# One group of an MLP's second products cut at token 512 in place of token 280

## The reference

```python
def _residual(x, mix, p):
    x = x + _rmsnorm(mix, p['g_post_mix'])
    f = jnp.square(jax.nn.relu(_rmsnorm(x, p['g_pre_mlp']) @ p['w_ff1'])) @ p['w_ff2']
    return x + _rmsnorm(f, p['g_post_mlp'])
```

## Time and profile before

| | |
|---|---|
| median of two runs | 2323.36 us |
| span of the profiled execution, first to last instruction | 2321.0 us |
| what lies around the span, against that median | 2.4 us |
| TensorE matmul busy | 2283.3 us (98%), 17472 records |
| weight loads busy (they overlap matmuls) | 2166.7 us (93%), 17472 records |
| VectorE, ScalarE, GpSimd busy | 916.8, 996.1, 935.4 us |
| mean granted clock of TensorE | 0.998 |

### The profile page before, as it was taken

One profiled execution on the slowest core, in us unless ns is written; L12 is line 12 of the kernel. 1 busy time (PEld: TensorE's weight loads), 2 busy tenths in 40 slices (PEclk: granted clock), 3 DMA queues, 4 the chain that ended last, 5 costly groups with the idle time before them and its releaser, 6 DMA issues.

```text
span 2321.0 us, 41258 instructions
## 1 busy us (share of the span) xinstructions
PE 2283.3 (98%) x17472; PEld 2166.7 (93%) x17472; DVE 916.8 (40%) x1909; ACT 996.1 (43%) x1879; POOL 935.4 (40%) x600
## 2 busy tenths in 40 slices
PE   7999999999999999999999999999999999999997
PEld 7999978889899999999999999788999999999997
DVE  6566555544514401001575664555344153000014
ACT  5444334443555642332344444344345556433412
POOL 2222224444665463544422223144455645545432
PEclk9999999999999999999999999999999999999999
DMA  5122221112124222222321222211222241222222
GB/s 195 54 64 62 85 76 59 57 62 74 62 82 155 68 83 91 82 90 66 118 88 53 72 62 90 70 58 56 72 65 65 82 167 55 83 91 82 90 80 72
DMA packets 59815, 187.89 MB, mean 81 GB/s; under 512 B 8400, under 2 KB 17552, under 8 KB 59120
## 3 DMA queue, kind: packets, MB, share of 16 engines
q1 hardware_dynamic: 51408, 169.28, 22.8%
q10 hardware_dynamic: 8224, 15.97, 1.9%
HBM read 170.99 MB, written 10.89 MB: 78 GB/s over the span
## 4 chain that ended last, share of the span: by engine, by line
PE 92%; DVE 5%; ACT 2%; issue 1%; DMA 0%; POOL 0%; SPq 0%; DVEq 0%
PE dense L941 43%; PE att L941 30%; PE att L1016 2%; PE att L1245 1%; PE att L1156 1%; PE att L1093 1%; PE att L1176 1%; PE att L1283 1%; PE dense L970 1%; PE att L1097 1%; PE att L1079 1%; PE att L1318 1%; DVE h_raw L1912 1%; PE att L1204 1%; PE att L1180 1%
## 5 line engine op out<-in xcount | busy, mean ns | idle before, releaser
L2304 POOL TENSOR_TENSOR wlo<-wraw,whi 128x1024 fp32r<-128x1024 f32 x245 | 588.2, 2408 | 596.9 <-ACT whi L1370 596.9
L941 PE MATMUL dense<-h_hi,whi 128*128 128x280 f32 x1888 | 556.5, 295 | 1.2 <-issue 0.9
L941 PE MATMUL dense<-h_lo,whi 128*128 128x280 f32 x1888 | 550.4, 292 | 0.0
L941 PE MATMUL dense<-h_hi,wlo 128*128 128x280 f32 x1888 | 549.2, 291 | 0.0
L1370 ACT ACTIVATE whi<-wraw 128x1024 fp32r<-128x1024 f32 x302 | 314.9, 1050 | 269.6 <-DMA wraw<-in_w 267.7
L941 PEld LDWEIGHTS dense<-h_hi,whi 128*128 128x128 f32 x1888 | 354.9, 188 | 14.5 <-issue 11.1
L941 PEld LDWEIGHTS dense<-h_hi,wlo 128*128 128x128 f32 x1888 | 354.4, 188 | 0.5
L941 PEld LDWEIGHTS dense<-h_lo,whi 128*128 128x128 f32 x1888 | 354.7, 188 | 0.0
L941 PE MATMUL att<-h_hi,whi 128*128 128x280 f32 x1024 | 299.3, 292 | 0.4 <-issue 0.4
L941 PE MATMUL att<-h_lo,whi 128*128 128x280 f32 x1024 | 298.3, 291 | 0.0
L941 PE MATMUL att<-h_hi,wlo 128*128 128x280 f32 x1024 | 297.8, 291 | 0.0
(11 more groups left out here) (366 smaller groups left out, 4584.3 us busy)
## 6 DMA issues: line engine op xcount, KB each, us to landing
wraw<-in_w SPq DMA_DIRECT2D x302, 512.0 KB, 3.6
x_spill<-x ACTq DMA_DIRECT2D x2, 2240.0 KB, 7.7
x<-x_spill ACTq DMA_DIRECT2D x2, 2240.0 KB, 12.0
k_cat<-k_rope SPq DMA_DIRECT2D x16, 212.0 KB, 3.4
x<-in_x SPq DMA_DIRECT2D x4, 560.0 KB, 6.3
out_y_out<-x SPq DMA_DIRECT2D x4, 560.0 KB, 3.1
out_c_out<-ckv SPq DMA_DIRECT2D x2, 560.0 KB, 5.4
state<-in_state ACTq DMA_DIRECT2D x8, 128.0 KB, 2.0
```

Of the source, the lines that this page charges most:

```text
L941: mm = pe.matmul(bank(u, o, hf)[0:m, :], a[:, k, o * 128:o * 128 + m], b[:, k, H[hf]], start=(k == 0 and i == 0), stop=(k == kt - 1 and i ...
L2304: pool.tensor_tensor(wlo[slot][:, :], wraw[slot][:, :], whi[slot][:, :].bitcast(F32), ALU.subtract).then_inc(pool_done, st.done("pool", f" ...
```

## The change

For `ff2` units 8 to 15 (group 1, in both layers) the two parts of tokens become 0 to 511 and 512 to 559. The six banks are taken at their full width of 512, and `bank` gives the first columns of one, as many as the part has. All other units keep their two parts of 280.

```diff
+CUT = SEQ
...
-        DENSE_BANKS = [dps[0][:, 0:HALF], dps[1][:, 0:HALF]] + [ps[:, b, 0:HALF] for b in (T0, T1, M_, O_)]
+        DENSE_BANKS = [dps[0][:, :], dps[1][:, :]] + [ps[:, b, :] for b in (T0, T1, M_, O_)]
...
+            def parts_of(u):
+                kind, n = UNITS[u]
+                return (slice(0, CUT), slice(CUT, T)) if kind == "ff2" and 8 <= n < 16 else H
...
             def bank(u, o, hf):
-                return bank_of[st.layer, u, o, hf]
+                part = parts_of(u)[hf]
+                return bank_of[st.layer, u, o, hf][:, 0:part.stop - part.start]
...
-                                    mm = pe.matmul(bank(u, o, hf)[0:m, :], a[:, k, o * 128:o * 128 + m], b[:, k, H[hf]],
+                                    mm = pe.matmul(bank(u, o, hf)[0:m, :], a[:, k, o * 128:o * 128 + m], b[:, k, parts_of(u)[hf]],
                                                    start=(k == 0 and i == 0), stop=(k == kt - 1 and i == 2))
...
-                            c = H[hf]
+                            c = parts_of(u)[hf]
```

## The result

The changed kernel takes 2367.07 us (median of two runs, 2366.52 and 2367.62) against 2323.36: 1.0191 times as long, 95% interval 1.0174 to 1.0208. It is slower, as forecast, but by 43.7 us in place of 29.5, and 1.1 us above the top of the range. The interval has 1.02 inside, so whether it is more or less than the two per cent of the prediction isn't decided.

The account below looks back on a forecast made before the run. TensorE's matmuls were taken to bound the kernel; 384 pairs of one wide (224.9 ns) and one narrow (108.5 ns) matmul, 76.8 ns more each, add 29.5 us, from 2323.4 to 2352.9 us, range 2348 to 2366 us.

Parts of the forecast that it names:

- the two per cent of the prediction: Whole kernel: 2% is what a measurement can tell from no change, 46.5 us or 2369.8 us; within it 87%.
- The bound: Group 1: TensorE and weight loads busy end to end, so each nanosecond per matmul reaches the program's end.
- the weights cost nothing: Group 1: slabs are asked for less often, ScalarE and GpSimd have room; VectorE's additions also costed at nothing.
- no wait gave anything back: In or behind group 1: no wait of TensorE that the delay could fill, so nothing comes back.
- The narrow matmul: Group 1's 48-wide matmuls: 108.5 ns each, set by a fresh load of 128 columns; upper bound 128.3 ns.
- The wide matmul: Group 1's 512-wide matmuls: 224.9 ns each, between 215.8 and 234.6 ns.
- today's 11.6 ns: 280-wide matmuls: 128.3 ns less 116.7 ns of streaming; taken as a fixed piece per matmul, not a slower stream.
- the sum: Group 1, both layers: a pair 333.4 ns in place of 256.6, times 384 pairs, +29.5 us.
- The clock: Group 1's narrow runs: no fall of the granted clock in the forecast, since earlier narrow runs stayed at 1.00.
- the clock falls: Rival, group 1: clock drops to 1.2 GHz in narrow runs or next wide runs, 2395 to 2431 us; chance 6%.
- The sign that the prediction names for it: Group 1's window in the new trace: a clock below 1.00 would mean the third rival, the clock falling.
- two thin stretches: Earlier trace: runs of 64-wide and 16-wide matmuls, 4.4 and 2.1 us, alone, where the clock stayed at 1.00.

Follow-up runs that it names:

- The halved load: Changed kernel with group 1's narrow matmuls using 64 of 128 columns of weights; 2336.61 us, 1.0060 times the kernel before.
- the 208 columns: Changed kernel with group 1's narrow part streaming 208 columns, of which the last 48 are taken out; 2355.80 us, 1.0143 times the kernel before.
- The two kernels that kept the full clock: Changed kernel with three wide and three narrow matmuls by turns, 2356.75 us; changed kernel with 208 columns streamed in the narrow part, 2355.80 us.
- the cut at 448: Changed kernel with group 1 cut into parts of 448 and 112 tokens in place of 512 and 48; 2345.63 us, 1.0098 times the kernel before.
- the runs of 48 matmuls: Changed kernel with units 9, 11, 13 and 15 taking their narrow part first, joining two narrow runs of 24; 2376.53 us, 1.0232 times the kernel before.

## Why the prediction was wrong

- **The bound** was right: TensorE stays the chain, VectorE's 0.69 and 0.20 us and the weights cost nothing, and no wait gave anything back.
- **The narrow matmul** was right in kind and a little small: 108.5 ns taken, 111.7 measured, 1.2 us over 384 of them. The halved load and the 208 columns show that it is the load. The Trainium skill's page "TensorE: Matmul & The Clock Gate", section "LDWEIGHTS (loading the stationary operand)", gives a load's time in ns as its columns divided by 1.2, by which 107 and 53 ns are estimates for 128 and 64; the traces agree within some 5 ns (111.7 and 58.1).
- **The wide matmul**: 224.9 taken, by which all of today's 11.6 ns are a fixed piece, from between 215.8 and 234.6 (all of it a slower stream); 230.8 measured, 2.3 us over 384. It is both: 4.6 ns fixed and 6% more than one cycle a column.
- Together the sum came to 33.0 us by these rates and 33.4 by the lengths of the units, where 29.5 stood. The two kernels that kept the full clock measured 34.1 and 33.2 (2356.75 and 2355.80 less the 2322.61 of the kernel before on their chip). That alone would have been in the range.
- **The clock** is the step that failed: the sum puts it at nothing, on the ground of the earlier trace rows. The rival "the clock falls" stood at 6%, priced as an every-unit affair of 42 to 78 us, so that the range took in nothing of it. What happened is a part of it: seven falls after sixteen narrow runs, each over the first wide matmuls of what follows, 11 us. The sign that the prediction names for it, a clock below 1.00 in the group's window, was there (0.91 over 961.40 to 1036.00 us). How far the time lies outside the range says little: two falls fewer, some 3.1 us, would have put it inside, with the same step missed. The argument against it was two thin stretches that kept the clock, one of which the earlier trace rows wasn't thin: its 64 plain float columns stream 53 of 108 ns, as much as the cut at 448 with 112 fp32r columns, which had no fall either. The other was shorter, 2.1 us, and alone. Neither was like a run of 20 ns in 112, 2.6 us long.
- The Trainium skill's page "TensorE: Matmul & The Clock Gate", "Part 1: The HAM clock gate", lets the clock go by how busy TensorE was of late. In this case busy in the profile's sense doesn't tell the two apart: the kernels of 48 and of 208 columns both show TensorE busy without a gap, with the same loads, and only the first falls. A run of loads with little streaming behind them didn't keep the clock up; how much a load counts by itself, no run here shows.

Why seven of the sixteen runs lead to a fall and not the other nine, with nothing different in their instructions, isn't settled. Only the size of that term depends on it: of the runs of 48 matmuls all eight led to a fall, of those with 208 columns none.

## What to carry to other kernels

In these runs a matmul that loads its own weights costs the longer of its load and its stream, so cut tokens into parts whose streams are all at least as long as the load (here some 242 columns of fp32r); a wider part saves nothing once it covers its load, and a narrow rest pays the load in full. Look at a thin run, one of much loading and little streaming, twice: what it costs itself, and what the clock that it leaves behind does to the thick run after it. If a narrow rest can't be avoided, put it between wide matmuls, or stream columns that nobody needs (2356.75 and 2355.80 us here, against 2367.07); either keeps the clock, neither saves the loads. A mean clock and a page's slices hide falls of a few microseconds; windows at the place of the change show them.

## What the runs showed of the hardware

- The granted clock went to half while TensorE had matmuls and loads in flight without a gap. With matmuls 48 wide, one every 111.7 ns, it did so after 7 of 16 runs of 24 and in or after 8 of 8 runs of 48; with 208 or 112 columns in the narrow part, in none of 16.
- Streaming 160 columns more in each of 384 matmuls made the program 10.5 us faster (33.2 against 43.7 us above the kernel before).
- An fp32r stream costs 4.6 ns and 0.442 ns a column at 2.4 GHz (128.3 ns at 280, 202.6 at 448, 230.8 at 512), a slope 6% over one cycle a column; the plain float rows 512 wide had 2.5 ns over two cycles a column.
- A fresh load ran ahead by one matmul only: the first narrow matmul after a wide one is followed after 20 ns, the next after some 111, in runs of 24 as in runs of three.
